# Sums of squares of the recurrence's output: one fp32 product against two fp32r products fed by ScalarE and GpSimd

## The chip, the cores and the metric

The kernel runs on one core of a Trainium2 chip. The metric is the device time of one execution in microseconds; of several runs the median counts.

## The reference

One encoder layer with two parallel branches over 1024 tokens of width 1024:

```
h = rmsnorm(x, norm_w)
proj = h @ w_in                       # 1024 x 5656, split among both branches and the gates
y_a = gated_deltanet(...)             # 8 heads of 64, chunks of 64 tokens
y_b = forgetting_attention(...)       # 8 heads of 64
merged = sigmoid(g_a) * (y_a @ w_up_gdn) + sigmoid(g_b) * (y_b @ w_up_fox)
out = rmsnorm(x + merged @ w_out, final_norm_w)
```

The change concerns the end of `gated_deltanet`. Over 16 chunks it carries a state, and each chunk gives an output `o`:

```
def step(state, xs):
    u = w_c - kc_c @ state
    o = qg_c @ state + a_c @ u
    state = state * gl_c + kt_c^T @ u
y = rmsnorm(o, norm_w) * silu(z)      # the mean of o*o over the 64 values of a head
```

For each token and head, `rmsnorm` needs the sum of 64 squares.

## The kernel before

All products with `w_in` are made on TensorE in fp32r, from a rounded high part and a low part of each operand: three matmuls of 128x512 for each 128 rows of the contraction (lines 144 to 146, in the records by tiles `pj<-h_hi,w_hi` and so on). One `fill` is such a group of three. After the q, k and v tiles are ready, the recurrence runs as a loop over t = 0 to 7 (called step t here), each step with 128 tokens, that is two chunks c = 0 and 1. All engines work through queues written out by hand, with semaphores between them, and TensorE takes its queue in order. In every step TensorE does, with fills strewn between:

- `from_state(t, c)`, L1143 and L1145: the state times the keys and the queries. It comes after s_done (the state) of the chunk before.
- `o_sums(t - 1)`, L1180: one fp32 product of a 128x128 matrix of two blocks of ones (`blk_ones`) with the squares of the step before (`vt`, 128x512), which gives the sums for all heads. It waits for `o_out`, the squares by ScalarE. Step 7's own product is made after the loop, after 2 fills, and 8 more fills end the block of code; there all engines meet.
- `through(t, c)`, L1157: the chunk's triangular inverse times its right-hand side. It waits for `r_step`, two VectorE operations (L923 and L927) on the result of `from_state`.
- `from_values(t, c)`, L1170 and L1173: the new state's increment and the rest of the output; it waits for VectorE's copy L929.

VectorE per chunk, in order: L918 (state times decay), L923 (PSUM result of `from_state` times a factor), L927 (subtract, both operands in SBUF), L929 (copy from PSUM), L933 (new state, one operand in PSUM). Between chunks its queue holds the sigmoid gate's L939 and L943 (in steps 1 to 4), a low part L132 of a weight tile (w_lo, in most steps), L949 (`o_scale`) and L955 (`o_gate`, of step 4 for four steps at once, 128x2048, and then for one, 128x512).

ScalarE at the end of a step takes the output out of PSUM (L717, waits `au_mm`), squares it (L720), and in the next step makes the reciprocal root of the sums (`o_norms`, L694 and L697, waits `ossq_mm`). It also takes fills' results (L569) and makes the high parts of weights (L128).

GpSimd makes masks at the start and four `affine_select`s of 128x2048 on the decay matrices (L475) before the recurrence, and has nothing to do during it.

Of the kernel before, what the change touches and what calls it, by code (L numbers as in the profile page):

```python
# [19 lines left out]
F32 = mybir.dt.float32  # L20
F32R = mybir.dt.float32r
I32 = mybir.dt.int32
ALU = mybir.AluOpType
ACT = mybir.ActivationFunctionType
ds = bass.ds

P = 128
HALF = 512
EPS = 1e-6
NEG = -1e30  # L30
LN_MAX = 1e18
DH = 64
C = 64
# [3 lines left out]
def program(nc, x, norm_w, w_in, gate_b, conv_w, a_log, dt_bias, gdn_norm_w, f_bias,  # L37
            fox_qn_w, fox_kn_w, fox_on_w, w_up_gdn, w_up_fox, w_out, final_norm_w, out):
    _, S, D = x.shape
    H = a_log.shape[1]  # L40
    KT = D // P
    NT = S // P
    PAIRS = H // 2
# [31 lines left out]
    with ctx:  # L75
        def sem(name):
            return ctx.enter_context(nc.semaphore(name))

        def sb(name, shape, dt=F32, where=ctx):
            return where.enter_context(nc.sbuf_tensor(name, shape, dt))  # L80
# [11 lines left out]
        w_hi = sb("w_hi", [P, 2, KT, P], F32R)  # L92
        w_lo = sb("w_lo", [P, 2, KT, P], F32R)
        ident = sb("ident", [P, P])
        blk_ones = sb("blk_ones", [P, P])
        cst = sb("cst", [P, P])
        vecs = sb("vecs", [P, 16])
# [50 lines left out]
                last.then_inc(pj_done, 1)  # L148

        outer = ctx.enter_context(ExitStack())  # L150
        qkv = sb("qkv", [P, QKV_T, S], where=outer)
        zg = sb("zg", [P, PAIRS, S], where=outer)
        st = outer.enter_context(ExitStack())
# [13 lines left out]
        state = sb("state", [P, 3, PAIRS, DH], where=st)  # L167

        qt, kt, vt = (qkv[:, PAIRS * n:PAIRS * (n + 1)] for n in range(3))
        xt, xs, nw_bc = qkv[:, 0:NT], qkv[:, NT:NT + 4], ebuf[:, :]  # L170
        u_row, e_row, sp_row, keep_row = (big[:, S * n:S * n + S] for n in range(4))
        crow = att[:, 0:S]
# [40 lines left out]
        kk_loaded = sem("kk_loaded")  # L213
        dk_spread = sem("dk_spread")
        de_spread = sem("de_spread")
        kept = sem("kept")
        dk_exp = sem("dk_exp")
        de_exp = sem("de_exp")
        de_stored = sem("de_stored")
# [63 lines left out]
        def tok_cols(t):  # L283

            return slice(P * t, P * t + P)
# [17 lines left out]
        def o_banks(t):  # L303

            return pc if t % 2 == 0 else pa
# [9 lines left out]
        with nc.Block() as block:  # L315
# [133 lines left out]
            @block.gpsimd  # L449
            def _(pool):  # L450
                made = [0]

                def link(ins):

                    made[0] += 1
                    ins.then_inc(masks, 1)
                    pool.wait_ge(masks, made[0])

                nc.gpsimd.memset(w_raw[:, 0], 0.0).then_inc(zeroed, 1)
                nc.gpsimd.memset(rows_in[:, :], 0.0).then_inc(zeroed, 1)  # L460
                link(nc.gpsimd.memset(ident[:, :], 0.0))
                link(nc.gpsimd.affine_select(ident[:, :], ident[:, :], pattern=[[-1, P]], base=0,
                                             channel_multiplier=1, compare_op=ALU.not_equal, fill=1.0))
                link(nc.gpsimd.memset(blk_ones[:, :], 0.0))
                link(nc.gpsimd.memset(blk_ones[0:DH, 0:DH], 1.0))
                link(nc.gpsimd.memset(blk_ones[DH:P, DH:P], 1.0))
                link(nc.gpsimd.memset(sel[:, :], 0.0))
                link(nc.gpsimd.memset(sel[0:DH, 0:1], 1.0))
                nc.gpsimd.memset(sel[DH:P, 1:2], 1.0).then_inc(masks, 1)

                def keep_lower(buf, made, keep):
                    for part in range(2):
                        rows = buf[:, 32 * part:32 * part + 32]
                        pool.wait_ge(made, part + 1)
                        nc.gpsimd.affine_select(rows, rows, pattern=[[-1, 32], [1, C]], base=-32 * part, channel_multiplier=0,  # L475
                                                compare_op=keep, fill=NEG).then_inc(kept, 1)

                keep_lower(dk, dk_spread, ALU.is_gt)
                keep_lower(de, de_spread, ALU.is_ge)

            @block.scalar
            def _(act):
# [131 lines left out]

                def exp_wide(buf, before, done):
                    for part in range(2):
                        act.wait_ge(kept, before + part + 1)
                        rows = buf[:, HALF * 4 * part:HALF * 4 * part + HALF * 4]
                        nc.scalar.activation(rows, rows, ACT.Exp).then_inc(done, 1)

                for n in range(1, N_CONV + 1):
                    take_qkv(n)
# [82 lines left out]
                for t in range(NT):  # L705
                    if 0 < t <= PAIRS:
                        z_exp(t - 1)
                    if t:
                        o_norms(t - 1)
                    if t % 2:  # L710
                        spill(halves_in(t)[0])
                    if 0 < t <= PAIRS:
                        z_sigmoid(t - 1)
                    if t % 2 == 0:
                        spill(halves_in(t)[0])
                    act.wait_ge(au_mm, 2 * t + 2)
                    nc.scalar.activation(by_bank(qt[:, :, tok_cols(t)]), o_banks(t)[:, :, 0:2 * P].rearrange("p g (a c) -> p g a c", c=P),  # L717
                                         ACT.Copy).then_inc(o_out, 1)
                    act.wait_ge(o_out, 2 * t + 1)
                    nc.scalar.activation(vt[:, :, tok_cols(t)], qt[:, :, tok_cols(t)], ACT.Square).then_inc(o_out, 1)  # L720
                    if t % 2:
                        spill(halves_in(t)[1])
                o_norms(NT - 1)
# [257 lines left out]
            def _(pe):  # L981
# [82 lines left out]
                for n in range(2, N_CONV + 1):  # L1064
                    project_tile(n)
                    if n == 6:
                        head_sums(0, k_sq)
                        kk(0)
                        kk(1)
                    if n == 7:  # L1070
                        kk(2)
                        kk(3)
                    if n == 11:
                        pe.wait_ge(tokq_done, 5)
                        pe.wait_ge(kk_out, 4)
                        perm = ident[:, :].rearrange("p (b a n) -> p b n a", b=2, a=PAIRS)
                        for b in range(2):
                            nc.tensor.matmul(pc[half_rows(b), 0, 0:C], tokq[:, 0], perm[:, b], start=True, stop=True)
                            nc.tensor.matmul(pc[half_rows(0), 0, chunk_cols(2 + b)], tokq[:, 2], perm[:, b],
                                             start=True, stop=True)  # L1080
                            for p in range(0, PAIRS, 2):
                                nc.tensor.matmul(pc[half_rows(side(b, p)), 0, C:2 * C].rearrange("p (n a) -> p n a", a=PAIRS)[:, :, p:p + 2],
                                                 tokq[:, 1], perm[:, b, :, p:p + 2], start=True, stop=True)
                        last = nc.tensor.matmul(pc[:, 1, 0:C].rearrange("p (n a) -> p a n", a=PAIRS), blk_ones[:, :],
                                                glr[:, 0].rearrange("p (a n) -> p a n", a=PAIRS), start=True, stop=True)
                        last.then_inc(tok_mm, 1)
                    if n == 10:
                        head_sums(1, q_sq)
# [32 lines left out]
                def fill(count):  # L1121

                    for _ in range(count):
                        tile, rest = divmod(done[0], 2 * KT)
                        project(pe, N_G + tile, (N_G + tile) % 2, rest // KT, rest % KT)
                        done[0] += 1
# [49 lines left out]
                    outs.then_inc(au_mm, 1)  # L1176

                def o_sums(t):
                    pe.wait_ge(o_out, 2 * t + 2)
                    nc.tensor.matmul(o_banks(t)[:, 0], blk_ones[:, :], vt[:, :, tok_cols(t)], start=True, stop=True).then_inc(ossq_mm, 1)  # L1180

                for t in range(NT):
                    fill(1)
                    from_state(t, 0)
                    fill(2)
                    if t:
                        o_sums(t - 1)
                    through(t, 0)
                    fill(1)
                    from_values(t, 0)  # L1190
                    fill(2)
                    from_state(t, 1)
                    fill(2)
                    through(t, 1)
                    fill(2)
                    from_values(t, 1)
                    fill(2)
# [232 lines left out]
        with nc.Block() as block:  # L1430
# [700 lines left out]
            def _(pe):  # L2131
# [173 lines left out]
                def square_sums(p, h):  # L2305
                    n = 2 * p + h
                    pe.wait_ge(u_step, 2 * n + 1 + h)
                    if h == 0:
                        pe.wait_ge(den_sq, 2 * p + 1)
                    elif p + 1 < PAIRS:  # L2310
                        pe.wait_ge(v_out, 2 * (p + 1) + 2)
                    nc.tensor.matmul(side_bank, blk_ones[:, :], usq[:, :], start=True, stop=True).then_inc(ss_mm, 1)  # L2312

                def turn_values(p, h):
                    if h == 0:
# [150 lines left out]
```

## Time and profile before

| what | value |
| --- | --- |
| median of 3 runs | 953.27 us (952.41 to 954.54) |
| the profiled execution | 954.61 us, span 952.8 us |
| TensorE matmul busy | 926.9 us, 97% of the span |
| VectorE, ScalarE, GpSimd busy | 611.3, 471.5 and 19.7 us |
| the recurrence (steps 0 to 7) | about 343 to 454 us from the span's start |
| TensorE's granted clock | full speed in all slices |

The busy share tells which engine is occupied; whether an operation lies on the path is to be read from the rows on what each engine waited for.

### The profile page before, as it was taken

The numbers are of one execution on the slowest core, as the hardware profiler recorded it, in microseconds if no ns is written. First come the engines' busy times: TensorE is split into PE (matmuls) and PEld (weight loads), VectorE is DVE, ScalarE is ACT, GpSimd is POOL, SyncE is SP. The second block draws the span as 40 slices with busy tenths as digits, with TensorE's granted clock in tenths as the row PEclk, the third lists the DMA queues.
The fourth block names the chain that finished last, engine by engine and source line by source line (L and its number), as shares of the span: only waits on it lengthen the run. The fifth ranks groups of instructions, "written<-read, shape, count | busy, mean of one in ns | idle before, by whom it ended". The sixth has DMA issues, their size and how long they took to land.

```text
span 952.8 us, 15910 instructions
## 1 busy us (share of the span) xinstructions
PE 926.9 (97%) x6380; PEld 699.5 (73%) x6380; DVE 611.3 (64%) x981; ACT 471.5 (49%) x842; POOL 19.7 (2%) x28
## 2 busy tenths in 40 slices
PE   5999999999999999999999999999999999999997
PEld 4778787888788876666765665666667888888885
DVE  7487668799999934464486786777863534246252
ACT  7555654532866625532647547466454543334131
POOL 1000002020000000000000000000000000000000
PEclk9999999999999999999999999999999999999999
DMA  7111451249223383322553326234125322223162
GB/s 251 43 48 45 102 170 47 68 170 205 91 89 112 108 255 93 101 73 94 131 183 101 100 100 166 89 99 134 35 67 159 105 91 76 68 111 111 39 195 76
DMA packets 115744, 104.87 MB, mean 110 GB/s; under 512 B 34192, under 2 KB 95760, under 8 KB 115288
## 3 DMA queue, kind: packets, MB, share of 16 engines
q1 hardware_dynamic: 104008, 80.27, 30.7%
q10 hardware_dynamic: 10512, 19.40, 5.5%
q0 software_dynamic: 1152, 4.19, 1.5%
q8 instruction: 51, 0.84, 0.4%
q14 instruction: 21, 0.17, 0.1%
HBM read 76.84 MB, written 27.00 MB: 109 GB/s over the span
## 4 chain that ended last, share of the span: by engine, by line
PE 47%; ACT 1%; DVE 1%; DMA 1%; issue 1%; SPq 0%; DVEq 0%; ACTq 0%
PE pj L2153 6%; PE pj L2155 6%; PE pj L2154 6%; PE pc L2286 3%; PE pa L2252 3%; PE pa L2221 2%; PE pj L2164 1%; PE pj L2166 1%; PE pj L2165 1%; PE pb L2312 1%; PE pb L2301 1%; PE pc L2419 1%; PE pc L2417 1%; PE pb L2419 1%; PE pb L2417 1%; PE pa L2419 1%
## 5 line engine op out<-in xcount | busy, mean ns | idle before, releaser
L144 PE MATMUL pj<-h_hi,w_hi 128*128 128x512 f32 x504 | 203.6, 404 | 0.5 <-DVE w_lo L132 0.5
L145 PE MATMUL pj<-h_lo,w_hi 128*128 128x512 f32 x504 | 196.9, 391 | 0.0
L146 PE MATMUL pj<-h_hi,w_lo 128*128 128x512 f32 x504 | 196.5, 390 | 0.0
L144 PEld LDWEIGHTS pj<-h_hi,w_hi 128*128 128x128 f32 x504 | 94.5, 188 | 23.9 <-issue 1.1
L146 PEld LDWEIGHTS pj<-h_hi,w_lo 128*128 128x128 f32 x504 | 94.6, 188 | 20.4
L145 PEld LDWEIGHTS pj<-h_lo,w_hi 128*128 128x128 f32 x504 | 94.7, 188 | 17.9 <-issue 0.2
L2153 PE MATMUL pj<-h_hi,w_hi 128*128 128x512 f32 x248 | 103.0, 415 | 0.3 <-PEq L315 0.3
L2155 PE MATMUL pj<-h_hi,w_lo 128*128 128x512 f32 x248 | 96.9, 391 | 0.0
L2154 PE MATMUL pj<-h_lo,w_hi 128*128 128x512 f32 x248 | 96.8, 390 | 0.0
L2153 PEld LDWEIGHTS pj<-h_hi,w_hi 128*128 128x128 f32 x248 | 46.5, 188 | 23.5 <-issue 14.5
L569 ACT ACTIVATE xc<-pj 128x512 f32<-128x512 f32 x39 | 23.3, 597 | 72.5 <-PE pj L146 71.8
L838 DVE TENSOR_TENSOR zg<-zg,tmp 128x62 f32<-128x62 f32 (+30 forms) x62 | 55.1, 889 | 2.1
L835 DVE TENSOR_TENSOR tmp<-zg 128x62 f32<-128x62 f32 (+30 forms) x62 | 55.1, 888 | 1.7
L2155 PEld LDWEIGHTS pj<-h_hi,w_lo 128*128 128x128 f32 x248 | 46.5, 188 | 10.2
L2154 PEld LDWEIGHTS pj<-h_lo,w_hi 128*128 128x128 f32 x248 | 46.6, 188 | 9.9 <-issue 1.4
L1957 DVE TENSOR_TENSOR fa<-fa 128x512 f32<-128x512 f32 (+3 forms) x80 | 39.0, 528 | 20.3 <-PE pc L2286 13.2
L132 DVE TENSOR_TENSOR w_lo<-w_raw,w_hi 128x1024 fp32r<-128x1024 f32 x33 | 40.2, 1220 | 13.2 <-ACT w_hi L128 13.2
L1661 ACT ACTIVATE fa<-pa,ccol 128x512 f32<-128x512 f32 (+3 forms) x48 | 27.5, 573 | 41.0 <-PE pc L2286 28.5
L809 DVE SCALAR_TENSOR_TENSOR qkv<-xc,cst,qkv 128x1024 f32<-128x1024 f32 x36 | 46.2, 1284 | 1.1
L128 ACT ACTIVATE w_hi<-w_raw 128x1024 fp32r<-128x1024 f32 x33 | 34.9, 1057 | 14.1 <-ACT xc L569 8.3
L662 ACT ACTIVATE qkv<-pc,tok 64x64 f32<-64x64 f32 x128 | 39.5, 309 | 1.5
L1629 ACT ACTIVATE gates<-pj,ngb 128x512 f32<-128x512 f32 x16 | 11.0, 685 | 58.8 <-PE pj L2155 58.8
(366 smaller groups left out, 1859.6 us busy)
## 6 DMA issues: line engine op xcount, KB each, us to landing
w_raw<-in_w_in SPq DMA_DIRECT2D x48, 512.0 KB, 4.4
fox_scratch<-xc ACTq DMA_DIRECT2D x39, 256.0 KB, 2.3
qkv<-in_x SPq DMA_DIRECT2D x8, 512.0 KB, 6.5
fa<-rows_scratch POOLq DMA_DIRECT2D x8, 512.0 KB, 5.1
rv<-fr_scratch SPq DMA_DIRECT2D x16, 256.0 KB, 4.2
ma<-m_scratch SPq DMA_DIRECT2D x8, 512.0 KB, 4.1
rv<-in_w_out SPq DMA_DIRECT2D x8, 512.0 KB, 4.5
w_raw<-in_x SPq DMA_DIRECT2D x8, 512.0 KB, 4.5
```

The source lines that it names most:

```text
L132: nc.vector.tensor_tensor(w_lo[:, slot], w_raw[:, slot], w_hi[:, slot].bitcast(F32), ALU.subtract).then_inc(w_ready, 1)
L144: nc.tensor.matmul(o, w_hi[:, slot, k], h_hi[:, k, cols], start=(k == 0), stop=False)
L145: nc.tensor.matmul(o, w_hi[:, slot, k], h_lo[:, k, cols], start=False, stop=False)
L146: last = nc.tensor.matmul(o, w_lo[:, slot, k], h_hi[:, k, cols], start=False, stop=(k == KT - 1))
L662: last = nc.scalar.activation(vt[half_rows(b), p, chunk_cols(x)], pc[half_rows(0), b, chunk_cols(PAIRS * (x % 2) + p)], ACT.Copy, scale=to ...
L809: nc.vector.scalar_tensor_tensor(y, src, tap, y, ALU.mult, ALU.add).then_inc(conv_step, 1)
L835: nc.vector.tensor_tensor(part, tm[:, j:j + 1, j + 1:C].broadcast_to([P, j, w]), tm[:, 0:j, j:j + 1].broadcast_to([P, j, w]), ALU.mult).th ...
L838: nc.vector.tensor_tensor(tm[:, 0:j, j + 1:C], tm[:, 0:j, j + 1:C], part, ALU.add).then_inc(m_step, 1)
L1957: nc.vector.tensor_tensor(total[h][hh][:, cols], total[h][hh][:, cols], weight[v % 2][hh][:, cols], ALU.add).then_inc(acc_done, 1)
L2153: nc.tensor.matmul(o, w_hi[:, n % 2, k], h_hi[:, k, cols], start=(k == 0), stop=False)
L2154: nc.tensor.matmul(o, w_hi[:, n % 2, k], h_lo[:, k, cols], start=False, stop=False)
L2155: last = nc.tensor.matmul(o, w_lo[:, n % 2, k], h_hi[:, k, cols], start=False, stop=(k == KT - 1))
```

## The change

`o_sums` becomes two fp32r products that accumulate: block ones times the squares rounded to fp32r (high part, `kt_r`, which lies in the place of the used-up keys), and block ones times the rest (low part, `vt_r`, in the place of the squares). ScalarE makes the high part with a further ACTIVATE Copy after the squares, GpSimd makes the low part with a `tensor_tensor` subtract of two SBUF operands, and TensorE waits for GpSimd. The block of ones is rounded once, in place, by ScalarE (`blk_r`); the two other products that use it read it with its bits taken as fp32 and are otherwise as before. In the loop `o_sums(t - 1)` stands one place later, after `through(t, 0)` and one fill. The semaphore `kept` is now `pool_part`, and counts the four selects and then the eight low parts.

```diff
+        with ExitStack() as same_place:
+            blk_r = sb("blk_r", [P, P], F32R, where=same_place)
         blk_ones = sb("blk_ones", [P, P])
...
+        with ExitStack() as same_place:
+            qkv_r = sb("qkv_r", [P, QKV_T, S], F32R, where=same_place)
         qkv = sb("qkv", [P, QKV_T, S], where=outer)
...
+        kt_r, vt_r = (qkv_r[:, PAIRS * n:PAIRS * (n + 1)] for n in (1, 2))
...
+                for t in range(NT):
+                    pool.wait_ge(o_out, 3 * t + 3)
+                    nc.gpsimd.tensor_tensor(vt_r[:, :, tok_cols(t)], vt[:, :, tok_cols(t)], kt_r[:, :, tok_cols(t)].bitcast(F32),
+                                            ALU.subtract).then_inc(pool_part, 1)
...
+                act.wait_ge(masks, 8)
+                nc.scalar.activation(blk_r[:, :], blk_ones[:, :], ACT.Copy)
...
-                    act.wait_ge(o_out, 2 * t + 1)
+                    act.wait_ge(o_out, 3 * t + 1)
                     nc.scalar.activation(vt[:, :, tok_cols(t)], qt[:, :, tok_cols(t)], ACT.Square).then_inc(o_out, 1)
+                    act.wait_ge(o_out, 3 * t + 2)
+                    nc.scalar.activation(kt_r[:, :, tok_cols(t)], vt[:, :, tok_cols(t)], ACT.Copy).then_inc(o_out, 1)
...
                 def o_sums(t):
-                    pe.wait_ge(o_out, 2 * t + 2)
-                    nc.tensor.matmul(o_banks(t)[:, 0], blk_ones[:, :], vt[:, :, tok_cols(t)], start=True, stop=True).then_inc(ossq_mm, 1)
+                    pe.wait_ge(pool_part, 4 + t + 1)
+                    nc.tensor.matmul(o_banks(t)[:, 0], blk_r[:, :], kt_r[:, :, tok_cols(t)], start=True, stop=False)
+                    nc.tensor.matmul(o_banks(t)[:, 0], blk_r[:, :], vt_r[:, :, tok_cols(t)], start=False,
+                                     stop=True).then_inc(ossq_mm, 1)
...
                     fill(2)
+                    through(t, 0)
+                    fill(1)
                     if t:
                         o_sums(t - 1)
-                    through(t, 0)
-                    fill(1)
                     from_values(t, 0)
```

On TensorE, in step 7 (the same holds for steps 1 to 6), the queue before has the product of sums, L1180, between the fills and `through`, L1157:

```order
L144 MATMUL pj<-h_hi,w_hi 128x512
L145 MATMUL pj<-h_lo,w_hi 128x512
L146 MATMUL pj<-h_hi,w_lo 128x512
L1180 MATMUL pc<-qkv,blk_ones 128x512 [waits o_out]
L1157 MATMUL pb<-qkv,tmp 64x64 [waits r_step,tt_loaded1]
L1157 MATMUL pb<-qkv,tmp 64x64 x7
L144 MATMUL pj<-h_hi,w_hi 128x512
L145 MATMUL pj<-h_lo,w_hi 128x512
L146 MATMUL pj<-h_hi,w_lo 128x512
L1170 MATMUL pb<-qkv,big 64x64 [waits qs_mm,u_done]
```

The same place of the changed kernel, in which lines 146 to 148 are the fills, L1172 is `through`, L1195 and L1196 are the two new products and L1185 is `from_values`:

```order
L146 MATMUL pj<-h_hi,w_hi 128x512
L147 MATMUL pj<-h_lo,w_hi 128x512
L148 MATMUL pj<-h_hi,w_lo 128x512
L1172 MATMUL pb<-qkv,tmp 64x64 [waits r_step,tt_loaded1]
L1172 MATMUL pb<-qkv,tmp 64x64 x7
L146 MATMUL pj<-h_hi,w_hi 128x512
L147 MATMUL pj<-h_lo,w_hi 128x512
L148 MATMUL pj<-h_hi,w_lo 128x512
L1195 MATMUL pc<-qkv_r,blk_r 128x512 [waits pool_part]
L1196 MATMUL pc<-qkv_r,blk_r 128x512
L1185 MATMUL pb<-qkv,big 64x64 [waits qs_mm,u_done]
```

`through` now follows the fills directly, and the products of sums stand behind it and a fill, just ahead of `from_values`.

On ScalarE, at the end of step 6 and the beginning of step 7, the queue before goes from the squares (L720) to the next step's `o_norms` (L694):

```order
L128 ACTIVATE w_hi<-w_raw 128x1024 [waits pj_done,w_loaded1]
L717 ACTIVATE qkv<-pc 128x4x128 [waits au_mm]
L720 ACTIVATE qkv<-qkv 128x4x128 [waits o_out]
L694 ACTIVATE qkv<-pc,vecs 128x4x128 [waits ossq_mm]
L697 ACTIVATE qkv<-qkv 128x4x128 [waits ors_done]
```

In the changed kernel L730 and L733 are the copy and the squares, L735 is the high part, and L707 and L710 are `o_norms`:

```order
L130 ACTIVATE w_hi<-w_raw 128x1024 [waits pj_done,w_loaded1]
L730 ACTIVATE qkv<-pc 128x4x128 [waits au_mm]
L733 ACTIVATE qkv<-qkv 128x4x128 [waits o_out]
L735 ACTIVATE qkv_r<-qkv 128x4x128 [waits o_out]
L707 ACTIVATE qkv<-pc,vecs 128x4x128 [waits ossq_mm]
L710 ACTIVATE qkv<-qkv 128x4x128 [waits ors_done]
```

One ACTIVATE has come between the squares and what follows them; GpSimd's subtract waits for it.

## Rows read from the trace of the kernel before

**Rows 1.** The page's parts 1 and 2: busy us of each engine; granted clock.
```profile
PE 926.9 (97%) x6380; PEld 699.5 (73%) x6380; DVE 611.3 (64%) x981; ACT 471.5 (49%) x842; POOL 19.7 (2%) x28
...
PEclk9999999999999999999999999999999999999999
```

**Rows 2.** Timeline, PE, step 7: start us, us, engine, line, what.
```profile
442.48 0.39 PE L146 MATMUL pj<-h_hi,w_lo 128*128 128x512 f32 x1
442.71 1.02 PE L1180 MATMUL pc<-qkv,blk_ones 128*128 128x512 f32 x2
443.66 0.46 PE L1157 MATMUL pb<-qkv,tmp 64*64 64x64 f32 x16
...
444.62 0.39 PE L146 MATMUL pj<-h_hi,w_lo 128*128 128x512 f32 x1
444.94 0.27 PE L1170 MATMUL pb<-qkv,big 64*64 64x64 f32 x1
```

**Rows 3.** Timeline, ACT, end of step 1.
```profile
370.24 0.64 ACT L720 ACTIVATE qkv<-qkv 128x512 f32<-128x512 f32 x1
```

**Rows 4.** Timeline, DVE, from step 1 to step 2.
```profile
371.10 1.22 DVE L132 TENSOR_TENSOR w_lo<-w_raw,w_hi 128x1024 fp32r<-128x1024 f32 x1
372.23 0.42 DVE L918 TENSOR_TENSOR state<-state,gl 128x256 f32<-128x256 f32 x1
372.57 0.42 DVE L923 TENSOR_TENSOR mq<-pb,tok 128x256 f32<-128x256 f32 x1
373.03 0.42 DVE L927 TENSOR_TENSOR qkv<-qkv,mq 128x256 f32<-128x256 f32 x1
```

**Rows 5.** Timeline, DVE, from step 4 to step 5.
```profile
412.70 2.29 DVE L955 TENSOR_TENSOR zg<-qkv,zg 128x2048 f32<-128x2048 f32 x1
...
415.70 0.43 DVE L927 TENSOR_TENSOR qkv<-qkv,mq 128x256 f32<-128x256 f32 x1
```

**Rows 6.** Timeline, PE: `through` of steps 1 (second chunk), 2 and 5.
```profile
366.82 0.46 PE L1157 MATMUL pb<-qkv,tmp 64*64 64x64 f32 x16 [1.24 <-DVE qkv L927]
...
374.77 0.34 PE L1157 MATMUL pb<-qkv,tmp 64*64 64x64 f32 x8
...
416.27 0.34 PE L1157 MATMUL pb<-qkv,tmp 64*64 64x64 f32 x8
```

**Rows 7.** Timeline, GpSimd's selects (POOL) and VectorE beside them.
```profile
148.75 3.08 POOL L475 TENSOR_SCALAR_AFFINE_SELECT big<-big 128x2048 f32<-128x2048 f32 x1 [145.09 <-DVE big L843]
...
148.62 1.23 DVE L822 TENSOR_TENSOR qkv<-qkv,ebuf 128x1024 f32<-128x1024 f32 x1
149.77 2.61 DVE L806 TENSOR_SCALAR qkv<-xc,cst 128x1024 f32<-128x1024 f32 x1
...
195.06 4.04 POOL L475 TENSOR_SCALAR_AFFINE_SELECT att<-att 128x2048 f32<-128x2048 f32 x1 [30.46 <-DVE att L843]
...
192.62 4.49 DVE L843 TENSOR_TENSOR att<-rr 128x2048 f32<-128x2048 f32 x2
197.03 2.14 DVE L835 TENSOR_TENSOR tmp<-zg 128x62 f32<-128x62 f32 x1
...
460.74 0.29 POOL L1570 TENSOR_SCALAR_AFFINE_SELECT mst<-mst 128x128 f32<-128x128 f32 x1
```

**Rows 8.** L806 by its line: ns min/median/max of its twelve.
```profile
L806 DVE TENSOR_SCALAR qkv<-xc,cst x12: 744/752/2607, 46.5 to 175.7; 128x1024 f32<-128x1024 f32 x12
```

**Rows 9.** Timeline, PE and ACT, after step 7.
```profile
453.52 1.11 PE L1180 MATMUL pa<-qkv,blk_ones 128*128 128x512 f32 x2
...
454.71 0.40 PE L145 MATMUL pj<-h_lo,w_hi 128*128 128x512 f32 x1
...
452.83 0.63 ACT L720 ACTIVATE qkv<-qkv 128x512 f32<-128x512 f32 x1
```

**Rows 10.** Timeline, ACT: two of its waits.
```profile
362.53 1.06 ACT L683 ACTIVATE ebuf<-zg 128x1024 f32<-128x1024 f32 x1 [6.65 <-DMA zg<-fox_scratch]
...
51.27 1.06 ACT L577 ACTIVATE ebuf<-qkv 128x1024 f32<-128x1024 f32 x1 [2.79 <-DVE qkv L809]
```

More of the change, by code:

```diff
@@ L215, in program @@
         de_spread = sem("de_spread")
-        kept = sem("kept")
+        pool_part = sem("pool_part")
         dk_exp = sem("dk_exp")
@@ L475, in keep_lower @@
                         nc.gpsimd.affine_select(rows, rows, pattern=[[-1, 32], [1, C]], base=-32 * part, channel_multiplier=0,
-                                                compare_op=keep, fill=NEG).then_inc(kept, 1)
+                                                compare_op=keep, fill=NEG).then_inc(pool_part, 1)
                 keep_lower(dk, dk_spread, ALU.is_gt)
                 keep_lower(de, de_spread, ALU.is_ge)
+                for t in range(NT):
+                    pool.wait_ge(o_out, 3 * t + 3)
+                    nc.gpsimd.tensor_tensor(vt_r[:, :, tok_cols(t)], vt[:, :, tok_cols(t)], kt_r[:, :, tok_cols(t)].bitcast(F32),
+                                            ALU.subtract).then_inc(pool_part, 1)
             @block.scalar
@@ L616, in exp_wide @@
                     for part in range(2):
-                        act.wait_ge(kept, before + part + 1)
+                        act.wait_ge(pool_part, before + part + 1)
                         rows = buf[:, HALF * 4 * part:HALF * 4 * part + HALF * 4]
                         nc.scalar.activation(rows, rows, ACT.Exp).then_inc(done, 1)
+                act.wait_ge(masks, 8)
+                nc.scalar.activation(blk_r[:, :], blk_ones[:, :], ACT.Copy)
                 for n in range(1, N_CONV + 1):
@@ L1083, in _ @@
                                                  tokq[:, 1], perm[:, b, :, p:p + 2], start=True, stop=True)
-                        last = nc.tensor.matmul(pc[:, 1, 0:C].rearrange("p (n a) -> p a n", a=PAIRS), blk_ones[:, :],
+                        last = nc.tensor.matmul(pc[:, 1, 0:C].rearrange("p (n a) -> p a n", a=PAIRS), blk_r[:, :].bitcast(F32),
                                                 glr[:, 0].rearrange("p (a n) -> p a n", a=PAIRS), start=True, stop=True)
@@ L2311, in square_sums @@
                         pe.wait_ge(v_out, 2 * (p + 1) + 2)
-                    nc.tensor.matmul(side_bank, blk_ones[:, :], usq[:, :], start=True, stop=True).then_inc(ss_mm, 1)
+                    nc.tensor.matmul(side_bank, blk_r[:, :].bitcast(F32), usq[:, :], start=True, stop=True).then_inc(ss_mm, 1)
                 def turn_values(p, h):
```

## The prediction

> **What bounds the kernel now.** I read the page first: TensorE is busy for 97% of the span at full clock in every slice, VectorE for 64%, ScalarE for 49%, GpSimd for 2% [rows 1]. So what TensorE saves counts in full, and so does each new idle moment on it. Then I went through the timeline of the recurrence engine by engine, and asked at each TensorE instruction that waits how long its input had been ready. For `through` (L1157) that is the end of VectorE's L927. Where TensorE really waited, it started 0.57 us after L927's start: 366.82 against 366.25, with an idle time of 1.24 us put down to L927 [rows 6]. That makes it start some 0.15 us after L927's end.
>
> **What is saved.** The fp32 product holds TensorE from 442.71 to 443.66, 0.95 us. A fill's matmul, fp32r and as wide, leads to the next start in 0.23 us (442.48 to 442.71) [rows 2], so two take 0.46. Counted with the changes of kind between wide and 64x64 matmuls (0.32 us from the last fill to L1170 [rows 2]), the step goes so: `through` could start at 442.80 in place of 443.66, 0.86 earlier; then as before until the fill's last matmul; the two products at +0.23 and +0.46; `from_values` 0.32 after, 1.74 us behind `through` in place of 1.28. Sum: -0.86 + 0.46 = -0.40 us a step, if nobody is late. Eight would be -3.2, but not all are to be had.
>
> **What is added on ScalarE.** An ACTIVATE of 128x512, for which I take that of the squares, 0.63 us [rows 3], 0.68 until GpSimd may start. In the steps it fits in ScalarE's waits. The rounding of the ones (128x128) falls in the 2.79 us in which ScalarE waits for VectorE at 51.27 [rows 10]; without that cover it would cost some 0.3. The later `o_norms` delay VectorE's L949, which still ends before the next chunk's L923 is wanted, and L569, whose PSUM half TensorE wants back eight fills later.
>
> **What GpSimd takes (call it T).** No subtract of two operands is in the trace. Selects with one input are: 128x128 in 0.29 us and 128x2048 in 4.04 - 2.0 = 2.04 us, once the time in which the 4.04 us row stood behind VectorE's L843 (until 197.1) is taken off [rows 7]. A line through both gives 0.64 us for 512 columns: the lower bound. Twice that, 1.28, is the upper, as if each operand cost a pass; with only the part per column doubled it is 1.1. I take 1.2. The Trainium skill, GPSIMD Engine Reference, section Elementwise, gives 4497 ns for a `tensor_tensor` add of 2048 fp32 columns, which would be an estimated 1.12 us for 512; with it the sum below would be 0.5 us less. No run here shows it yet.
>
> **GpSimd and VectorE shut each other out.** That is the point on which I think the sum turns. L806 takes 0.75 us by its median and 2.61 us where it starts at 149.77 under a select: it ends at 152.38, 0.55 after the select's end (151.83) [rows 7, 8]. The select itself took 3.08 in place of 2.04 because it had to wait for L822 to end at 149.85, an operation with two SBUF operands. And L835, 62 columns wide, takes 2.14 us: it was issued at 197.03, the select that had been waiting since 195.06 got in ahead of it, and it ended 0.07 us after that select (199.10) [rows 7]. So the one that asks first goes first, to its end, and a held VectorE operation ends about 0.15 to 0.2 us sooner after its release than its own duration says. The Trainium skill states this of SBUF — State Buffer, section Who interferes with whom: a VectorE instruction with two SBUF inputs and a GpSimd instruction that reads SBUF exclude each other for the whole instruction. By that rule, the trace agrees (2.61 us against 0.75); without it the time would be that of rival 2 below.
>
> L132, L943, L955, L918 and L927 have two SBUF operands, L923, L929 and L933 one. GpSimd asks 1.31 us after the squares' start in each step. Step by step, as a shift of TensorE against before:
>
> - Step 1: its second `through` waits for VectorE, VectorE for ScalarE, ScalarE for the z rows by DMA until 362.53 [rows 6, 10]. The 0.40 won is spent waiting there. Shift 0.
> - Step 2: GpSimd asks at 371.55, L132 holds until 372.32 [rows 4], GpSimd runs until 373.52, L918 ends at 373.76 (+0.24), L923 starts at 373.68, L927 0.46 later at 374.14, `through` at 374.71, against 374.77 before [rows 6] and 373.91 wanted. Shift -0.06, and +0.40 at `from_values`.
> - Step 3: the same behind L132 of step 2: a stall of 0.77, shift +0.77.
> - Step 4: no VectorE work in the way, L927 in time: -0.40, shift +0.37.
> - Step 5: L955, 128x2048, holds until 414.99 [rows 5]; already before, `through` at 416.27 was as late as L927 (415.70) allowed [rows 5, 6], so the 0.86 can't be had. GpSimd runs to 416.56 with the shift, L927 starts at 417.18, `through` at 417.75: shift +1.48, then +1.94.
> - Steps 6 and 7: GpSimd stands behind L955 of 128x512 and ends 1.2 after it; stalls of 0.17 and 0.22; shift +1.71, then +1.53.
> - After step 7 only two fills cover the chain. Before, the product started at 453.52, as soon as the squares (452.83 + 0.63) were there [rows 9]. Now 0.63 for the high part, 1.2 for GpSimd and 0.06 for its signal come on top: 1.89 later, and 0.48 us less for the product itself (the fill's L145 at 454.71 [rows 9] goes by this pair's start). +1.41, and it is all on the path, since the rest is eight fills and the meeting of the engines.
>
> **Sum:** 0 + 0.40 + 0.37 - 0.40 + 1.57 - 0.23 - 0.18 + 1.41 = +2.9 us: span 955.7 against 952.8 (the profiled execution 954.6 to 957.5; it lies 1.3 above the median, so on the median 953.3 to 956.2). T enters about six times: at 0.64 us the sum is +0.3, at 1.28 +3.4. That I can't tell less than 0.2%, 1.9 us, from no change applies to all that follows.
>
> **The rivals.**
> 1. VectorE's queued L918 goes ahead of GpSimd, and only L927 is held. For it: L918 is issued before the operation ahead of it has ended. Against it: L835 was issued so too and lost [rows 7]. Price: by the same arithmetic -0.12, -0.11, -0.40, +1.11, -0.40, -0.40 for steps 2 to 7 and +1.41 at the end: +1.1 us, 954.4.
> 2. No exclusion for this instruction, so that the change does at each place what it saves. For it: L822 (1.23 us, as its like) wasn't stretched by a select beside it [rows 7]. Against it: the select was. Price: -0.40 in five steps (2, 3, 4, 6, 7), but +0.46 in step 5, where L927 comes behind the big L955 as before, and +1.41 at the end: -0.1 us, 953.1, and with T = 0.64 -0.7, 952.6. This is the one that ends not slower. It decides if VectorE's L918 and L927 keep their 0.42 us.
> 3. GpSimd much slower, say T = 2.0 us, since two operands and four pieces of 128 columns are unlike a select, or its first subtract late: six terms of +0.8: +7.7, 961.0. Nothing in the trace speaks for it but that the operation is missing there.
>
> **How the numbers follow.** The likeliest, exclusion with T from 1.0 to 1.4: 0.54, at +1.7 to +4.1, of which 0.47 over the bound of 1.9. Rival 1: 0.17. Rival 2: 0.12, and I add 0.04 that something I don't see makes it faster by over 0.2%. Rival 3: 0.13. So faster 0.04, same 0.36 (0.07 + 0.17 + 0.12), slower 0.60. The range of 953.0 to 959.0 takes in rival 2 and leaves out the 0.04 and the worse part of rival 3, T above some 1.7 us; the likeliest one's own range is 955.0 to 957.4.
>
> **What would show it.** Right: POOL rows of about 1.2 us after steps 3 and 7, up to 2 us or more where they wait behind L132 or L955 (steps 1, 2, 4); VectorE's L918 of 1.3 to 1.6 us in steps 2, 3 and 5; an idle TensorE ahead of `through` in steps 2 and 3 by 0.8 and in step 5 by 2.0 us; 1.9 us of waiting for GpSimd ahead of the last product; pairs of products with 0.23 us between starts. Wrong: L918 and L927 at 0.42 throughout, a POOL row of 0.7 or 2 us at the end of step 7, or waits of `o_sums` for GpSimd inside the loop, where I count 2 us of room.

## The result: slower by half a per cent

| | median | runs | ratio to the kernel before, 95% interval |
| --- | --- | --- | --- |
| before | 953.27 us | 5 (952.24 to 955.87) | |
| the change | 958.64 us | 5 (955.92 to 959.82) | 1.0049 (1.0032 to 1.0065) |
| the change again, beside the experiments | 958.67 us | 6 (958.19 to 961.73) | 1.0065 (1.0051 to 1.0079) |

The change makes the kernel slower by some 5 us; 2.9 us were forecast. The profiled execution of the change is its fastest run, 955.92 us with a span of 954.1 us.

The page of the changed kernel, parts 1 and 2 (compare [rows 1]):

```profile
PE 925.8 (97%) x6380; PEld 701.1 (73%) x6380; DVE 616.8 (65%) x981; ACT 476.0 (50%) x851; POOL 32.9 (3%) x36
...
POOL 1000002020000000110100000000000000000000
```

TensorE is busy for 1.1 us less and yet the kernel is longer. GpSimd has 13.2 us more, in eight subtracts (L488), one for each step. The timeline of POOL shows five of them (start us, us, line, what):

```profile
369.54 1.85 POOL L488 TENSOR_TENSOR qkv_r<-qkv,qkv_r 128x512 fp32r<-128x512 f32 x1 [11.99 <-ACT qkv_r L735]
...
397.63 1.28 POOL L488 TENSOR_TENSOR qkv_r<-qkv,qkv_r 128x512 fp32r<-128x512 f32 x1 [12.20 <-ACT qkv_r L735]
411.27 3.09 POOL L488 TENSOR_TENSOR qkv_r<-qkv,qkv_r 128x512 fp32r<-128x512 f32 x1 [12.36 <-ACT qkv_r L735]
428.02 1.28 POOL L488 TENSOR_TENSOR qkv_r<-qkv,qkv_r 128x512 fp32r<-128x512 f32 x1 [13.66 <-ACT qkv_r L735]
...
454.96 1.26 POOL L488 TENSOR_TENSOR qkv_r<-qkv,qkv_r 128x512 fp32r<-128x512 f32 x1 [12.19 <-ACT qkv_r L735]
```

Alone it takes 1.26 us (after step 7). In step 1 it takes 1.85 and in step 4 3.09. The times after step 7 and in step 4 (454.96 and 411.27) are those behind the last squares and behind the squares of step 4. The timeline of VectorE shows what stood in its way and whom it then held up. The lines have moved: L933, L938, L942 and L944 are the L918, L923, L927 and L929 of before, L134 is L132, and L970 is L955.

```profile
369.02 1.22 DVE L134 TENSOR_TENSOR w_lo<-w_raw,w_hi 128x1024 fp32r<-128x1024 f32 x1
370.15 1.52 DVE L933 TENSOR_TENSOR state<-state,gl 128x256 f32<-128x256 f32 x1
...
372.04 0.43 DVE L942 TENSOR_TENSOR qkv<-qkv,mq 128x256 f32<-128x256 f32 x1
...
410.94 2.29 DVE L970 TENSOR_TENSOR zg<-qkv,zg 128x2048 f32<-128x2048 f32 x1
413.15 1.49 DVE L933 TENSOR_TENSOR state<-state,gl 128x256 f32<-128x256 f32 x1
```

L134 ends at 370.24, GpSimd at 371.39, 1.15 later, and L933, issued at 370.15, lasts 1.52 us in place of 0.42 and ends at 371.67. With L970 it is the same: L970 ends at 413.23, GpSimd at 414.36, L933 at 414.64. What this does to TensorE, compared with [rows 2, 6, 9], is in its timeline:

```profile
372.61 0.29 PE L1172 MATMUL pb<-qkv,tmp 64*64 64x64 f32 x4 [0.71 <-DVE qkv L942]
...
373.81 0.39 PE L1195 MATMUL pa<-qkv_r,blk_r 128*128 128x512 f32 x1
374.04 0.40 PE L1196 MATMUL pa<-qkv_r,blk_r 128*128 128x512 f32 x1
...
415.58 0.29 PE L1172 MATMUL pb<-qkv,tmp 64*64 64x64 f32 x4 [1.95 <-DVE qkv L942]
...
456.28 0.50 PE L1195 MATMUL pa<-qkv_r,blk_r 128*128 128x512 f32 x1 [1.84 <-POOL qkv_r L488]
456.61 0.40 PE L1196 MATMUL pa<-qkv_r,blk_r 128*128 128x512 f32 x1
```

The pair inside the loop is as cheap as counted (0.23 us between its starts) and waits for nobody. But `through` has idle time ahead of it, and the last pair waits 1.84 us for GpSimd.

The part that was not forecast is in the stretches of the window view (busy us of PE, PEld, DVE, ACT and POOL; then the granted clock, the share of DMA, GB/s):

```profile
416.00:417.00 1.00, 1.00 (x7) 0.83 (x5) 0.42 (x1) 0.00 (x0) 0.00 (x0) 1.00 0.06 16
417.00:421.00 4.00, 4.00 (x40) 2.75 (x38) 1.36 (x3) 2.72 (x4) 0.00 (x0) 0.57 0.17 66
421.00:424.00 3.00, 3.00 (x57) 2.26 (x57) 1.08 (x3) 0.14 (x1) 0.00 (x0) 1.00 0.01 3
```

Before, the clock stood at its upper level, 2.4 GHz, in all these slices. Now it falls to the lower one, 1.2 GHz, for about 3.4 of the four us, beginning some 1.6 us after the idle time of 1.95 us at 415.58 ended.

**Measuring a few microseconds.** Spans differ by 1 to 2 us for reasons outside the recurrence (when the z rows land, for one). So I compare, besides the medians, the time on TensorE from the second `through` of step 1 to the first matmul of the next block. All differences of the change lie in it but for step 1's own pair, whose 0.40 us the prediction took to be lost in a wait. Before it goes from 366.82 [rows 6] to 460.43, 93.61 us; with the change from 364.74 to 462.79, 98.05 us:

```profile
364.74 0.29 PE L1172 MATMUL pb<-qkv,tmp 64*64 64x64 f32 x4
...
462.79 0.47 PE L2170 MATMUL pj<-h_hi,w_hi 128*128 128x512 f32 x1 [0.33 <-PEq L320]
```

The two profiled spans differ by only 1.3 us (952.8 and 954.1), because this profile of the change is 2.1 us shorter ahead of the stretch, where its `through` of step 1 had no wait as the 1.24 us before [rows 6], and 1.1 us shorter behind it. That the change costs some 5 us is read from the medians.

### The profile page after: what moved, and what is told of

Its sections match the earlier page's. It is cut to its first block, busy times and chain, and to the rows that moved or that the text cites. A ratio compares the mean times of both kernels' runs of the same rounds, so it can differ in the third digit from the quotient of the medians.

```text
span 954.1 us, 15927 instructions
## 1 busy us (share of the span) xinstructions
PE 925.8 (97%) x6380; PEld 701.1 (73%) x6380; DVE 616.8 (65%) x981; ACT 476.0 (50%) x851; POOL 32.9 (3%) x36
## 4 chain that ended last, share of the span: by engine, by line
PE 47%; ACT 1%; DVE 1%; DMA 1%; issue 0%; SPq 0%; DVEq 0%; ACTq 0%
PE pj L2170 6%; PE pj L2172 6%; PE pj L2171 6%; PE pc L2303 3%; PE pa L2269 2%; PE pa L2238 2%; PE pj L2181 1%; PE pj L2183 1%; PE pj L2182 1%; PE pb L2329 1%; PE pb L2318 1%; PE pc L2436 1%; PE pc L2434 1%; PE pb L2436 1%; PE pb L2434 1%; PE pa L2436 1%
## 5 line engine op out<-in xcount | busy, mean ns | idle before, releaser
L134 DVE TENSOR_TENSOR w_lo<-w_raw,w_hi 128x1024 fp32r<-128x1024 f32 x33 | 40.2, 1219 | 11.9 <-ACT w_hi L130 11.9
```

What stands on the lines that cost most here:

```text
L134: nc.vector.tensor_tensor(w_lo[:, slot], w_raw[:, slot], w_hi[:, slot].bitcast(F32), ALU.subtract).then_inc(w_ready, 1)
```

## The experiments

All medians and ratios are against the kernel before on the same chip. "Stretch" is the time just defined, in the profiled execution; "low clock" counts how often the clock was at half within it, about 3.4 us each time.

| kernel | median us (before beside it) | ratio, 95% interval | stretch against 93.61 | low clock |
| --- | --- | --- | --- | --- |
| the change | 958.64 (953.27) | 1.0049 (1.0032 to 1.0065) | +4.4 | 1 |
| e0, the change again | 958.67 (953.35) | 1.0065 (1.0051 to 1.0079) | +6.1 | 2 |
| e1, subtract later | 954.05 (953.35) | 1.0015 (0.9997 to 1.0034) | +1.8 | 1 |
| e2, no subtract | 951.97 (953.35) | 0.9989 (0.9979 to 0.9998) | -1.4 | 0 |
| e3, step 4 as before | 956.46 (953.35) | 1.0035 (1.0021 to 1.0049) | +2.3 | 0 |
| e4, step 7 as before | 955.87 (953.12) | 1.0036 (1.0022 to 1.0050) | +1.4 | 0 |
| e5, e1 and step 7 as before | 952.86 (952.93) | 0.9991 (0.9977 to 1.0005) | -1.4 | 0 |
| e6, old place | 954.70 (952.93) | 1.0023 (1.0006 to 1.0040) | +2.8 | 1 |
| e7, before with the load | 954.34 (952.93) | 1.0015 (0.9998 to 1.0032) | +1.1 | 0 |
| e8, only step 7 changed | 955.64 (952.93) | 1.0026 (1.0013 to 1.0039) | +3.2 | 1 |
| e9, e5 and step 4 as before | 951.31 (953.12) | 0.9984 (0.9972 to 0.9996) | -2.2 | 0 |

**e0: the change again.** No edit.

> The changed kernel once more, as the yardstick of this chip. In the profile of the change, the idle times ahead of `through` in steps 2, 3 and 5 (0.71, 0.71 and 1.95 us) and 1.84 us ahead of the last product come out as forecast (+2.9 us in sum), but the timed runs were 4.7 to 5.4 us slower, at a mean granted clock of 0.993 to 0.998, and the profile shows TensorE at 0.5 for some 3 us behind the 1.95 us stall. Theory A (exclusion of GpSimd and VectorE makes the stalls, and the clock falls behind the long one): again +4 to +5.5 us over the kernel before, with a clock below 1.000 in the profile and a low stretch within a few us of step 5. Rival B (the clock dip is chance): a clock of 1.000 in the profile and +2.5 to +3.5 us.

Measured: +5.3 us in the median, timed clocks of 0.993 to 0.998, and in the profile two stretches at the low clock, one behind the stall of step 5 and one behind the stall after step 7:

```profile
418.00:422.00 4.00, 4.00 (x42) 2.87 (x41) 1.06 (x3) 1.80 (x3) 0.00 (x0) 0.66 0.00 0
...
457.00:462.00 5.00, 4.36 (x12) 3.45 (x13) 1.38 (x2) 1.32 (x2) 0.58 (x1) 0.66 0.14 52
```

Both speak against rival B, which had a clock of 1.000 and +2.5 to +3.5 us. The cost of a low stretch can be read here too: from the `through` of step 5 to that of step 6 it is 14.97 us (416.92 to 431.89), as in the change (14.95).

**e1: GpSimd's subtract later.**

```diff
                     pool.wait_ge(o_out, 3 * t + 3)
+                    if t + 1 < NT:
+                        pool.wait_ge(r_step, 4 * t + 6)
```

> The change with one wait more: GpSimd's subtract of step t also waits for r_step of the next step's first chunk, so that it starts when VectorE's L918, L923 and L927 are through, and runs beside operations with at most one SBUF tensor operand. Theory A: L918 back to 0.42 us in all steps, no idle time ahead of `through` but for some 0.75 us in step 5 (L955 of 128x2048), a clock of 1.000, and -0.40 in steps 2, 3, 4, 6 and 7, +0.46 in step 5 and +1.5 after step 7: -0.1 us against the kernel before (-0.6 to +0.7). Rival C (the cost is the product's new place and the longer chain to the sums, not the exclusion): +2.5 us or more, since both stay, and the product would come to wait for GpSimd inside the loop.

Of VectorE's state-times-decay (L933 in the change, L935 here) the view by line gives ns min/median/max:

```profile
L935 DVE TENSOR_TENSOR state<-state,gl x16: 416/418/424, 334.9 to 444.2; 128x256 f32<-128x256 f32 x16
```

and the timeline has GpSimd's subtract of step 1's squares without a wait in it, now behind L944 (the change's L942):

```profile
372.16 1.28 POOL L490 TENSOR_TENSOR qkv_r<-qkv,qkv_r 128x512 fp32r<-128x512 f32 x1 [12.89 <-DVE qkv L944]
```

No L935 is over 0.424 us; in the change the longest of its 16 was 1.535. The stretch is +1.8 with one low clock behind the last stall, which is 1.5 of it (e4 has the price), so +0.3 where -0.1 was expected. Some 0.2 of the difference is in step 5, where the pair waits a moment for GpSimd, which ends at 414.88 (the pair starts at 414.93). The median, +0.7, is at the edge of the expected range, and its interval (0.9997 to 1.0034) does not tell it from no change. Rival C, with +2.5 us or more, is out: later place and longer chain are all still there.

**e2: no subtract.** The low part is left out; the high part is multiplied twice.

```diff
-                for t in range(NT):
-                    pool.wait_ge(o_out, 3 * t + 3)
-                    nc.gpsimd.tensor_tensor(vt_r[:, :, tok_cols(t)], vt[:, :, tok_cols(t)], kt_r[:, :, tok_cols(t)].bitcast(F32),
-                                            ALU.subtract).then_inc(pool_part, 1)
...
-                    pe.wait_ge(pool_part, 4 + t + 1)
+                    pe.wait_ge(o_out, 3 * t + 3)
                     nc.tensor.matmul(o_banks(t)[:, 0], blk_r[:, :], kt_r[:, :, tok_cols(t)], start=True, stop=False)
-                    nc.tensor.matmul(o_banks(t)[:, 0], blk_r[:, :], vt_r[:, :, tok_cols(t)], start=False,
+                    nc.tensor.matmul(o_banks(t)[:, 0], blk_r[:, :], kt_r[:, :, tok_cols(t)], start=False,
```

> The change without GpSimd's subtract: TensorE waits for the high part alone and multiplies the high part twice, so the low part is left out and the sums are twice too large. Theory A: no exclusion anywhere and only 0.67 us more to wait after step 7, less 0.48 for the cheaper product: -0.40 in five steps, +0.46 in step 5, +0.2 at the end: -1.3 us against the kernel before (-0.8 to -2.0), clock 1.000. Rival C (placement, ScalarE's extra operation): +1 us or more remains.

Measured: -1.4 us in the median and in the stretch (-1.3 expected), and the longest of the 16 state-times-decays takes 0.424 us. ScalarE's added operation and the new place are still there, so they are not what costs. The last pair waits only for the high part, by the view of waits (us in total, times, longest):

```profile
PE pa L1191 <- ACT qkv_r L731: 0.5, 1, 0.5
```

**e3: step 4 as before.** The sums of step 4 by the fp32 product in the new place, without the two new operations (`OLD = (4,)`; the counts waited for follow).

```diff
...
-                    pe.wait_ge(pool_part, 4 + t + 1)
+                    if t in OLD:
+                        pe.wait_ge(o_out, outs_before(t) + 2)
+                        nc.tensor.matmul(o_banks(t)[:, 0], blk_r[:, :].bitcast(F32), vt[:, :, tok_cols(t)], start=True,
+                                         stop=True).then_inc(ossq_mm, 1)
+                        return
+                    pe.wait_ge(pool_part, parts_at(t))
```

> The change, but the sums of step 4 by the one fp32 product as before (in the new place) and without ScalarE's and GpSimd's part in that step. Theory A: the idle time ahead of `through` in step 5 falls from 1.95 to about 0.75 us, with it the dip of the clock: a profile clock of 1.000 and +2.1 to +2.6 us against the kernel before, that is 2 to 3 us under e0, of which only 0.7 is the stall (1.2 less, 0.48 for the dearer product). Rival B (the dip is chance and does not hang on this stall): 0.7 us under e0, with the same clocks as e0 in the timed runs. Rival D (the dip comes behind any of the stalls, step 2 to 7): it moves to another step.

The stall of step 5 is 0.88 us (expected 0.75) in the timeline (L1182 is `through` here and in e4, L952 the change's L942), and the clock stays up in the whole loop and, in this execution, behind the last stall too, by the window view:

```profile
415.27 0.46 PE L1182 MATMUL pb<-qkv,tmp 64*64 64x64 f32 x16 [0.88 <-DVE qkv L952]
```

```profile
454.00:460.00 6.00, 5.13 (x23) 4.25 (x24) 1.39 (x2) 1.32 (x2) 0.82 (x1) 1.00 0.11 44
```

The stretch is +2.3 us, as expected. The median is 2.2 us under e0, within the 2 to 3 of theory A and not the 0.7 of rival B, but at +3.1 over the kernel before it is above the +2.6 at most that I had expected; its eight runs spread from 954.58 to 958.98 us at mean clocks of 0.994 to 0.998, so in some of them the clock may have fallen behind the last stall. Of rival D this much is true: low stretches come behind the last stall as well (e0, e1, e6, e8), but none came behind the stalls of 0.7 us.

**e4: step 7 as before.** As e3 with `OLD = (7,)`.

> The change with the sums of step 7 by the one fp32 product as before, the loop unchanged. Theory A: the end's share is gone and the loop's stays: +2.0 us (0.48, 0.45, -0.40, 1.65, -0.13, -0.1) against the kernel before, and 1.5 us more in the executions in which the clock falls behind the 1.95 us stall of step 5: +2.0 to +3.5 in the median, about 2 to 3 us under the whole change. If the loop's stalls cost nothing in the end, it would be within 0.7 us of the kernel before.

The timeline and the window view of the place where the change's clock fell:

```profile
417.22 0.46 PE L1182 MATMUL pb<-qkv,tmp 64*64 64x64 f32 x16 [1.95 <-DVE qkv L952]
```

```profile
417.00:421.00 4.00, 3.78 (x59) 2.83 (x59) 1.46 (x4) 1.80 (x3) 0.00 (x0) 1.00 0.02 4
```

The same stall of 1.95 us as in the change, and this time the clock stayed up. So this profile and the change's have the loop alike but for the dip, and price it: from the `through` of step 5 to that of step 6 it is 13.47 us here (417.22 to 430.69) and 14.95 in the change (415.58 to 430.53), so a dip costs 1.48 us. Two more readings come near it: e0's first dip, 14.97 in the same place, 1.50, and e0's second, 20.39 us from the `through` of step 7 to the next block (445.36 to 465.75) against 18.79 in the change, 1.60. The median of +2.8 us lies in the expected range, the stretch at +1.4 below the +2.0 expected: each hold-up was 1.13 to 1.16 us and not the 1.28 that I had put in.

**e5: e1 and step 7 as before.**

> As e1 (GpSimd's subtract waits until the next chunk's L927 is through), and the sums of step 7, after the loop, by the one fp32 product as before, without the high and low part. Theory A: the 1.84 us stall after step 7 and with it the low stretch of the clock behind it are gone; left are -0.40 in five steps and +0.46 in step 5: -1.5 us against the kernel before (-0.8 to -2.2), with a clock of 1.000 in the profile between 340 and 700 us. If the 3.4 us of half clock came by chance and not behind the stalls, it shows here as often as in e1, and the time is nearer to -0.5.

The stretch is -1.4 us and the clock is up throughout the recurrence, so no dip comes where no long stall is left; the ratio of 0.9991 (0.9977 to 1.0005) does not tell it from no change, nor from the -1.5 expected.

**e6: old place.** The pair back ahead of `through`.

```diff
                     fill(2)
+                    if t:
+                        o_sums(t - 1)
                     through(t, 0)
                     fill(1)
-                    if t:
-                        o_sums(t - 1)
```

> The change without its move: the pair of products stands ahead of `through`, where the fp32 product stood. Theory A, by the same arithmetic with T = 1.28 us: GpSimd holds L918 back as before, but TensorE reaches `through` 0.46 later, so the delay of L927 is covered in steps 2 and 3 (shift 0, in place of +0.4 each), step 4 gains 0.40, step 5 ends at +0.8 (stall about 1.3 us), step 6 at +0.4, step 7 at 0, and the end adds 1.5: +1.5 us against the kernel before, 2 us under e0, and more than that if the 1.3 us stall does not pull the clock down as the 1.95 us one did. Rival E (the move is what saves, since it gives GpSimd its time): the products would wait for GpSimd inside the loop and the time would be above e0's.

The timeline of TensorE at the beginning of step 5:

```profile
414.16 0.50 PE L1195 MATMUL pc<-qkv_r,blk_r 128*128 128x512 f32 x1 [0.78 <-POOL qkv_r L488]
...
415.33 0.46 PE L1172 MATMUL pb<-qkv,tmp 64*64 64x64 f32 x16 [0.44 <-DVE qkv L942]
```

The long stall of step 5 has become two short ones of 0.78 and 0.44 us (1.3 expected). The stretch is +2.8 with one dip behind the end, so +1.3 without (1.5 expected), and the median +1.8. The move one place later, which was to give GpSimd time, therefore cost 1.6 us: it took from `through` the 0.86 us of cover that L942 (L927 before) now needed. Rival E is half true: in step 5, behind the big L955, the pair does wait for GpSimd, but the whole is shorter.

**e7: the kernel before with the load.** ScalarE's copy and GpSimd's subtract are added and their result is not used.

```diff
...
+                for t in range(NT):
+                    pool.wait_ge(o_out, 3 * t + 3)
+                    nc.gpsimd.tensor_tensor(kt_r[:, :, tok_cols(t)], vt[:, :, tok_cols(t)], kt_r[:, :, tok_cols(t)].bitcast(F32),
+                                            ALU.subtract).then_inc(kept, 1)
...
+                    act.wait_ge(kept, 4 + t + 1)
...
+                    act.wait_ge(o_out, 3 * t + 2)
+                    nc.scalar.activation(kt_r[:, :, tok_cols(t)], vt[:, :, tok_cols(t)], ACT.Copy).then_inc(o_out, 1)
...
```

> The kernel before, TensorE's queue untouched, with ScalarE's high part and GpSimd's subtract added as a mere load (their result is overwritten by the root of the sums, which now also waits for GpSimd; the sums are those of the kernel before). Theory A: L918 takes 1.5 us behind L132 and L955, `through` has 0.86 us of room in steps 2, 3, 6 and 7 and keeps its time there, and only step 5 loses: +1.2 us against the kernel before (+0.7 to +1.7), with one stall of about 1.2 us. Rival C (GpSimd's work costs nothing by itself, the loss is in TensorE's queue): 0.

The timeline of VectorE between steps 1 and 2 (L929 is the state times decay here), and of TensorE at the `through` of steps 2 and 5:

```profile
371.65 1.51 DVE L929 TENSOR_TENSOR state<-state,gl 128x256 f32<-128x256 f32 x1
```

```profile
374.17 0.34 PE L1168 MATMUL pb<-qkv,tmp 64*64 64x64 f32 x7
...
416.76 0.29 PE L1168 MATMUL pb<-qkv,tmp 64*64 64x64 f32 x4 [1.10 <-DVE qkv L938]
```

GpSimd's work holds up VectorE just as in the change (1.51 us), without TensorE's queue being touched. In step 2 it is covered (no idle time ahead of 374.17); in step 5 it costs 1.10. The stretch is +1.1 and the median +1.4, as expected (+0.7 to +1.7), though the interval of the ratio (0.9998 to 1.0032) just reaches no change; that GpSimd's work holds up VectorE rests on the rows.

**e8: only step 7 changed.** As e3 with `OLD = (0, ..., 6)`, in the old place.

> The kernel before (fp32 product, old place) for steps 0 to 6, and the change for step 7 alone, after the loop. Theory A: one stall, 1.84 us ahead of the last pair, worth +1.9 less 0.48 for the cheaper pair: +1.5 us with the clock at 1.000, and 1.7 us more (3.41 us at half clock) in those executions in which the clock falls behind it; so a median of +1.5 to +3.2 and timed runs that lie in two clusters. If it is 0 to +0.7, the end of the loop is covered by something that I don't see.

The timeline of the last pair, and the window behind it:

```profile
454.44 0.50 PE L1210 MATMUL pa<-qkv_r,blk_r 128*128 128x512 f32 x1 [1.83 <-POOL qkv_r L497]
```

```profile
455.00:459.00 4.00, 4.00 (x12) 3.12 (x11) 1.38 (x2) 1.32 (x2) 0.00 (x0) 0.57 0.02 7
```

The stretch is +3.2, of which 1.5 the dip: +1.7 for the stall (1.5 expected), and the median is +2.7. The two clusters that I expected of the timed runs are not to be seen (954.35 to 956.94 without a gap); how often the clock fell in them is open.

**e9: e5, and step 4 by the old product in the old place** (`OLD = (4, 7)`). The part that differs from e5:

```diff
+                    if t and t - 1 in OLD:
+                        o_sums(t - 1)
                     through(t, 0)
                     fill(1)
-                    if t:
+                    if t and t - 1 not in OLD:
                         o_sums(t - 1)
```

> GpSimd's subtract waits until the next chunk's L927 is through, as in e1; the sums of step 7 by the one fp32 product after the loop and those of step 4 by it in its old place ahead of `through` (step 5's `through` is late anyway, because of L955 of 128x2048). Theory A: -0.40 in five steps and 0 in steps 1, 5 and 7's end: -2.0 us against the kernel before (-1.3 to -2.6), 0.5 us under e5, no stall over 1.3 us and no low clock between 340 and 470 us. At most a measurable gain of 0.2%; if it is the same as the kernel before, the fp32r pairs' 0.40 us a step are given back somewhere after the recurrence.

The window from step 0 to the end of the loop, at full clock, and by the view of waits the two waits for L954 (the change's L942) that are left, 1.1 us in sum:

```profile
345.00:455.00 110.00, 107.90 (x1560) 77.50 (x1561) 55.03 (x104) 48.30 (x67) 7.65 (x6) 1.00 0.39 105
```

```profile
PE pb L1184 <- DVE qkv L954: 1.1, 2, 0.8
```

951.31 us against 953.12, ratio 0.9984 (0.9972 to 0.9996), stretch -2.2: this version beats the kernel before by 1.8 us and the change by some 7 us, by what the pairs save where nothing takes it back.

## Why the prediction held, point by point

The stalls and their sizes came out as forecast. The median did not: of its +5.3 us, the prediction's mechanism gives 3.0, and the rest is a cost that it did not have. That 958.64 still lay inside the range, 0.4 us from its end, is luck: the upper part of the range had been left for a slower GpSimd (rival 3), not for the clock.

**The saving.** Two fp32r products in place of one fp32: -0.40 us a step was forecast. In step 4, where nobody is late, the distance from the `through` of step 3 to that of step 4 is 13.27 us (386.65 to 399.92), against 13.65 before: -0.38. e9, which keeps it in five steps, has -2.2 where -2.0 was summed.

**GpSimd's time.** Forecast 1.2 us between bounds of 0.64 and 1.28; it is 1.26 to 1.28 where the way was free and 1.13 to 1.16 from the end of the VectorE operation that it had waited for. The upper bound, twice the one-operand line, was the near one.

**Exclusion.** As forecast: VectorE's two-operand L918 is held until GpSimd has ended (1.52, 1.51 and 1.49 us in steps 2, 3 and 5 for 0.42, and 1.53 in steps 6 and 7), GpSimd until L132 or L955 has ended. Taking GpSimd's work away (e2) or to another time (e1) takes it away; adding it to the kernel before (e7) makes it. By the Trainium skill, SBUF — State Buffer, section Who interferes with whom, a VectorE instruction with two SBUF inputs and a GpSimd instruction that reads SBUF shut each other out for the whole instruction. The trace of the change agrees for the subtract as well (1.52 us against 0.42). L938, with one SBUF operand, started in the middle of the subtract that ran from 397.63 to 398.91 and kept its time:

```profile
398.45 0.42 DVE L938 TENSOR_TENSOR mq<-pb,tok 128x256 f32<-128x256 f32 x1 [0.92 <-PE pb L1158]
```

One reading of the prediction does not bear this out: the row by which it said that the trace agrees, L806 with 2.61 us for 0.75, is an operation with one tensor operand. The row on two operands was the select that waited for L822. Why L806 was held by a select and L938 not by the subtract, no run here shows. Rivals 1 and 2 were wrong, and rival 3 too.

**The terms.** Against forecasts for T = 1.2 us of +0.40, +0.37, -0.40, +1.57, -0.23, -0.18 and +1.41, taken at `from_values`, I read the distances between the first `through`s of the steps in the change's profile, less those before, which hold the same terms cut at another place. From the second `through` of step 1 to that of step 2: -0.08 (forecast -0.06); then +0.31 (+0.37), -0.38 (-0.40), +1.54 (+1.57), +1.21 (-0.23), -0.18 (-0.18), and to the next block +2.02 (+0.46 and +1.41). Only step 5 to 6 is off, by 1.44 us: the clock. Without the dip the stretch would be 4.44 - 1.48 = +2.96 us; the forecast was +2.9.

**What was missing: the clock.** The prediction took TensorE's clock as constant, on the strength of its row before [rows 1], and priced each stall at its length. The runs showed that a stall of 1.8 to 1.95 us brings a price of its own. Of nine such stalls in the profiles (two in the change, two in e0, one each in e1, e3, e4, e6 and e8) six were followed by a low stretch at 1.2 GHz, three (one in the change, e3, e4) were not; and in the recurrence of kernels whose stalls there are no longer than 1.3 us (before, e2, e5, e7, e9) the clock never fell. Nor did it fall anywhere else between 20 and 945 us in the twelve profiles, so the dips are not spread by chance. What sets whether a given stall brings one stays open. In the timed runs of e0 the mean clock is 0.9948, of the kernel before beside it 0.9979. Over some 957 us the difference is 3.0 us of full clock, and since each us at half clock lacks half a us, that is 5.9 us at half clock, 1.7 dips, an estimated 2.6 us of time. It is an upper estimate, because the mean also counts low clock that costs nothing, at the very end of the span, where TensorE has finished (0.4 us in the profile of the kernel before, 3.2 in e0's). With +2.96 it makes up to +5.5, and the median's +5.3 is covered. The result was above the likeliest case's own range of 955.0 to 957.4.

**Where the gain went.** Of the 0.40 us that five steps could have kept, steps 2 and 3 each lost all and about 0.4 us more to the exclusion, and steps 6 and 7 about half. Step 5 ended 1.5 us worse than before: 0.5 of it is there without the exclusion too (e1: 14.59 us from the `through` of step 4 to that of step 5 against 14.12 before), since `through` could not start earlier behind the big L955, and 1.1 is the exclusion. The end lost 1.6 us by an ordinary chain: the high part (0.66) and GpSimd (1.26) between the squares and a product that has two fills of cover.

## What to carry to other kernels

An idle GpSimd isn't free help for a busy VectorE: here each subtract held up the two-operand SBUF instruction of VectorE that came up beside it, and waited for the one ahead of it, so the longest of these adds to the delay. Ask what VectorE has queued at the moment GpSimd will ask, and start it where VectorE works out of PSUM (e1). Where both the cover and the product move, count whose cover is taken: moving the pair later gave its own chain time that it needed only in step 5, and took 0.86 us of cover from `through`, which cost 1.6 us (e6). And price a new stall on a TensorE that is otherwise never idle above its length, when it comes near 2 us.

## What the runs showed of the hardware that I had not expected

A single idle time of 1.8 to 1.95 us on a TensorE busy for 97% of the span was followed in six of nine cases by 3.4 us at half clock, for 1.48 us of loss, beginning 0.4 to 1.6 us after its end, although matmuls ran without a gap from there on; whether a given stall does it changes from one execution to the next of the same kernel (the 1.84 us one in the change did not, in e0 it did). GpSimd's 128x512 subtract of two SBUF operands took 1.13 to 1.16 us from the end of a VectorE instruction that it had waited for, and 1.26 to 1.28 us when it found the way free.
